# High weights against both parts of the rows in one 512-column product, in the gate and up chunks of a feed-forward block

## The reference

```
def swiglu(h, w_gate, w_up, w_down):
    return (jax.nn.silu(h @ w_gate) * (h @ w_up)) @ w_down

f = swiglu(rms_norm(h, ffn1_pre_g[l]), ffn1_w_gate[l], ffn1_w_up[l], ffn1_w_down[l])
h = h + FFN_RESIDUAL_SCALE * rms_norm(f, ffn1_post_g[l])
```

## Time and profile before

| what | value |
|---|---|
| time, median of 3 runs | 1905.47 us (1904.33 to 1905.68) |
| the profiled execution | 1905.51 us, its span 1903.5 us |
| mean granted TensorE clock | 0.951 of full speed |
| PE busy | 1800.9 us (95%), 12512 matmuls |
| DVE busy | 1123.6 us (59%) |
| ACT busy | 793.8 us (42%) |
| DMA | 297.33 MB, mean 156 GB/s |

### The profile page before, as it was taken

The page is one execution under the profiler, slowest core; times in us unless marked ns, Lnnn a source line. Parts: engine busy times, 40 slices in busy tenths (PEclk is TensorE's granted clock), DMA queues, the critical chain, the costliest instruction groups (busy, mean ns, idle before and its releaser), DMA issues.

```text
span 1903.5 us, 28797 instructions
## 1 busy us (share of the span) xinstructions
PE 1800.9 (95%) x12512; PEld 1667.4 (88%) x12512; DVE 1123.6 (59%) x1315; ACT 793.8 (42%) x1009; POOL 42.6 (2%) x64
## 2 busy tenths in 40 slices
PE   7999997999999999999999799999999998879987
PEld 6999897898898999899989789889899987668765
DVE  5444689654357444744568965435744478647763
ACT  5333633443345333533353345334533454444442
POOL 0000000000000000000000000000000010001000
PEclk9999999798899999999999979979999999889979
DMA  7555544233255555545555423324555553215210
GB/s 276 178 194 182 199 178 155 89 133 133 90 177 199 179 192 182 204 179 190 186 196 181 155 89 133 133 89 166 194 195 178 191 201 123 89 44 209 96 66 22
DMA packets 43037, 297.33 MB, mean 156 GB/s; under 512 B 4768, under 2 KB 5152, under 8 KB 8352
## 3 DMA queue, kind: packets, MB, share of 16 engines
q1 hardware_dynamic: 39744, 285.23, 41.4%
q10 hardware_dynamic: 3168, 10.26, 1.5%
HBM read 294.42 MB, written 1.05 MB: 155 GB/s over the span
## 4 chain that ended last, share of the span: by engine, by line
PE 75%; DVE 10%; ACT 6%; issue 5%; DVEq 2%; POOL 1%; DMA 1%; ACTq 0%; POOLq 0%; SPq 0%
PE ps L1347 21%; PE ps L1348 21%; PE ps L1349 21%; DVE wlo L816 3%; DVE mix L1015 2%; ACT whi L525 2%; PE ps L1715 2%; PE ps L1742 2%; PE ps L1579 1%; PE ps L1574 1%; ACT prob L786 1%; PE ps L1433 1%; PE ps L1581 1%; POOL rs L486 1%; PE ps L1726 1%
## 5 line engine op out<-in xcount | busy, mean ns | idle before, releaser
L816 DVE TENSOR_TENSOR wlo<-raw,whi 128x2048 fp32r<-128x2048 f32 x270 | 616.5, 2290 | 445.8 <-ACT whi L525 434.3
L1347 PE MATMUL ps<-xhi,whi 128*128 128x256 f32 x2496 | 724.9, 290 | 5.2 <-DVE wlo L816 5.0
L1348 PE MATMUL ps<-xlo,whi 128*128 128x256 f32 x2496 | 717.5, 287 | 0.0
L1349 PE MATMUL ps<-xhi,wlo 128*128 128x256 f32 x2496 | 716.8, 287 | 0.0
L525 ACT ACTIVATE whi<-raw 128x2048 fp32r<-128x2048 f32 x270 | 509.2, 1906 | 17.5 <-DMA raw<-stream 16.9
L1347 PEld LDWEIGHTS ps<-xhi,whi 128*128 128x128 f32 x2496 | 491.4, 197 | 15.4 <-DVE wlo L816 7.0
L1348 PEld LDWEIGHTS ps<-xlo,whi 128*128 128x128 f32 x2496 | 491.0, 197 | 2.6 <-issue 0.6
L1349 PEld LDWEIGHTS ps<-xhi,wlo 128*128 128x128 f32 x2496 | 490.4, 196 | 0.0
L1347 PE MATMUL ps<-whi,yar 128*128 128x512 f32 (+1 forms) x492 | 195.9, 398 | 0.7 <-DVE wlo L816 0.7
L1348 PE MATMUL ps<-wlo,yar 128*128 128x512 f32 (+1 forms) x492 | 192.1, 390 | 0.0
L1349 PE MATMUL ps<-whi,yar 128*128 128x512 f32 (+1 forms) x492 | 191.4, 389 | 0.0
(11 more groups left out here) (202 smaller groups left out, 1896.8 us busy)
## 6 DMA issues: line engine op xcount, KB each, us to landing
raw<-stream SPq DMA_DIRECT2D x270, 1024.0 KB, 4.8
gpre<-pre_gain ACTq DMA_DIRECT2D x9, 512.0 KB, 4.2
gpost<-post_gain ACTq DMA_DIRECT2D x6, 512.0 KB, 5.0
h<-x_in SPq DMA_DIRECT2D x2, 512.0 KB, 5.9
out<-mix SPq DMA_DIRECT2D x4, 256.0 KB, 2.0
cst<-cst_in ACTq DMA_DIRECT2D x1, 704.0 KB, 12.1
cst<-cst_in ACTq DMA_DIRECT2D x1, 576.0 KB, 6.7
par<-par ACTq DMA_DIRECT2D x2, 271.0 KB, 5.5
```

The lines of the kernel that those rows point to most:

```text
L816: TT(wlo[:, s, :], raw[:, s, :], whi[:, s, :].bitcast(F32), ALU.subtract).then_inc(lo_v, 1)
L1347: pe.matmul(dst, lh, rh, start=first, stop=False)
L1348: pe.matmul(dst, lh, rl, start=False, stop=False)
L1349: return pe.matmul(dst, ll, rh, start=False, stop=last)
```

## The change

`xhi` and `xlo` become the two halves of one tile `xhl`, side by side for each slice k. For groups 2 to 10 of every feed-forward stage (18 chunks a stage, 72 in all), `features_wide` takes the place of `features`: the high weights multiply both halves in one matmul of 512 columns, then the low weights multiply the high half in one of 256 columns into the first half of the same bank. Each half m has now a bank of its own: gate goes to banks 2 and 3, up to banks 0 and 1. The sum of the two halves of each bank is left to DVE, as a reduction over pairs: `gate_sum` in the second half of `thb`, `up_sum` in the second half of `tmp`. ACT takes silu of `gate_sum` instead of PSUM. TensorE waits for the reductions of the group before instead of silu and product.

```diff
+            def features_wide(ch, b):
+                s = ch % SLOTS
+                wh, wl = wts(whi, s, KD), wts(wlo, s, KD)
+                for m in range(2):
+                    w = slice(m * P, (m + 1) * P)
+                    for k in range(KD):
+                        pe.matmul(bank(b + m), wh[:, k, w], xhl[:, k, :, :].rearrange("p a t -> p (a t)"),
+                                  start=(k == 0), stop=False)
+                        ins = pe.matmul(bank(b + m)[:, 0:T], wl[:, k, w], xhi[:, k, :], start=False, stop=(k == KD - 1))
+                ins.then_inc(used, 1)
...
                 def gate_up(c, g):
                     ready(c)
-                    pe.wait_ge(silu_done, f * NG + g)
-                    features(c, 0)
+                    if g > 2:
+                        pe.wait_ge(gate_done, f * (NG - 2) + (g - 2))
+                    features_wide(c, 2)
                     ready(c + 1)
-                    pe.wait_ge(prod_done, f * NG + g)
-                    features(c + 1, 1)
+                    if g > 2:
+                        pe.wait_ge(up_done, f * (NG - 2) + (g - 2))
+                    else:
+                        pe.wait_ge(prod_done, f * NG + 2)
+                    features_wide(c + 1, 0)
...
             def ffn(ch, f):
+                def gate(c, g):
+                    if g < 2:
+                        return
+                    chunk_used(dve, c)
+                    dve.wait_ge(silu_done, f * NG + g)
+                    dve.tensor_reduce(gate_sum, ps[:, 2:4, :].rearrange("p m (a t) -> p m t a", a=2), AX,
+                                      ALU.add).then_inc(gate_done, 1)
+
                 def up(c, g):
+                    if g < 2:
+                        dve.wait_ge(silu_done, f * NG + g + 1)
+                        chunk_used(dve, c)
+                        TT(prod, silu, bank(1), ALU.mult).then_inc(prod_done, 1)
+                        return
+                    chunk_used(dve, c)
+                    dve.tensor_reduce(up_sum, ps[:, 0:2, :].rearrange("p m (a t) -> p m t a", a=2), AX,
+                                      ALU.add).then_inc(up_done, 1)
+                    dve.drain()
                     dve.wait_ge(silu_done, f * NG + g + 1)
-                    chunk_used(dve, c)
-                    TT(prod, silu, bank(1), ALU.mult).then_inc(prod_done, 1)
+                    TT(prod, silu, up_sum.rearrange("p m t -> p (m t)"), ALU.mult).then_inc(prod_done, 1)
...
                 for g in (NG - 2, NG - 1):
                     c = ch + FFN_CH - 7 + 2 * (g - (NG - 2))
+                    gate(c, g)
                     split(c + 3)
                     up(c + 1, g)
                     hidden(g)
...
                 def silu_of(g, c):
-                    chunk_used(act, c)
+                    if g < 2:
+                        chunk_used(act, c)
+                    else:
+                        act.wait_ge(gate_done, f * (NG - 2) + (g - 1))
                     if g:
                         act.wait_ge(prod_done, f * NG + g)
-                    A(silu, bank(0), ACT.Silu).then_inc(silu_done, 1)
+                    src = bank(0) if g < 2 else thb[:, 512:1024]
+                    A(silu, src, ACT.Silu).then_inc(silu_done, 1)
```

More of the change, by code:

```diff
@@ L236, in program @@
         h = sb("h", [P, NT, D])
-        xhi = sb("xhi", [P, KD, T], F32R)
-        xlo = sb("xlo", [P, KD, T], F32R)
+        xhl = sb("xhl", [P, KD, 2, T], F32R)
+        xhi, xlo = xhl[:, :, 0, :], xhl[:, :, 1, :]
         mix = sb("mix", [P, 11456])
@@ L300, in program @@
         th2 = thb[:, 512:1024]
+        gate_sum = thb[:, 512:1024].rearrange("p (m t) -> p m t", m=2)
+        up_sum = tmp[:, 512:1024].rearrange("p (m t) -> p m t", m=2)
         lat_hi = yar[:, 0, 0:768].rearrange("p (m t) -> p m t", m=3)
@@ L360, in program @@
         prod_done = sem("prod_done")
+        gate_done = sem("gate_done")
+        up_done = sem("up_done")
         ht_done = sem("ht_done")
```

## The result

| | before | after |
|---|---|---|
| time, median (range, runs) | 1905.54 us (1902.65 to 1913.18, 8) | 1915.33 us (1911.08 to 1919.01, 8) |
| ratio, 95% interval | | 1.0049 (1.0031 to 1.0066) |
| profiled execution | 1905.51 us, span 1903.5 | 1915.33 us, span 1913.5 |
| mean granted clock | 0.951 | 0.949 |

A forecast was written before the change was run, and what follows sets the result against it. The prediction took TensorE's pace, busy 95% of the span, as the bound. It summed 1905.51 - 15.6 + 12.6 + 3.9 = 1906.4 us, likeliest range 1902 to 1910, 8 in 10 from 1899 to 1917.

The forecast's parts named there:

- PE in the 72 wide chunks: TensorE in groups 2 to 10: a chunk takes 5.54 us instead of 5.76, saving 15.6 us in four stages.
- I take the rows' value: Wide chunks' 512-column matmul: assumed 0.2265 us, as in down chunks, though no row showed it with alternating bank halves.
- DVE and ACT in groups 2 to 8: Two added reductions a group, 1.22 us each, are hidden in the 16.55 us period and cost nothing.
- The last two groups: Groups 9 and 10 of each stage: reductions delay the last down chunk's split, 3.15 us a stage, +12.6 us.
- Nothing is won back: Stage end: after the late last split, DVE's boundary and TensorE both move by the same 3.15 us.
- The clock: TensorE's 3.5 us wait at stage ends drops the clock, 1.3 us in three of four stages, +3.9 us.
- Slow reduction: Rival, DVE in the last two groups: a reduction over pairs takes 2.29 us, giving 1923.5 us; chance 0.12.
- fast reduction: Rival, stage ends: a reduction takes 0.69 us, TensorE waits only 1.6 us, clock holds, 1894.8 us; chance 0.10.
- The clock holding: Rival: the clock stays full through the waits at stage ends, giving 1902.5 us; chance 0.20.
- The wide matmul saving nothing: Rival, wide chunks: they stay at 5.76 us, the fixed part not being saved, giving 1919.5 us; chance 0.08.
- The estimate from the Trainium skill: Merging two matmuls saves about 2.5 ns each over 1152 matmuls, 2.9 us; it spoke against the change.
- the likeliest case: The forecast itself for the whole kernel, 1906.4 us, own range 1902 to 1910 us; chance 0.50.

The follow-up runs named there:

- e4: The changed kernel with each half's 8 matmuls of 512 columns together, then its 8 of 256, instead of turn about; 1909.63 us, ratio 1.0025 to the kernel before.
- e5: The changed kernel with the narrow matmul adding into the second half of its bank instead of the first; 1915.78 us, one run.
- e6: The changed kernel with weight splits ahead in groups 9 and 10 and low weights multiplying both halves, so all wide-chunk matmuls have 512 columns; 2010.49 us, one run.
- e1: The changed kernel with wide products in groups 2 to 8 only, groups 9 and 10 as before; 1897.99 us, ratio 0.996 to the kernel before.
- e2: The changed kernel with wide products in groups 9 and 10 only, groups 2 to 8 as before; 1924.46 us, ratio 1.009 to the kernel before.
- e3: The changed kernel, all 72 chunks wide, with weight splits ahead of silu and reduction in groups 9 and 10; 1894.03 us, ratio 0.9945 to the kernel before.
- e7: The kernel before with only the weight splits moved ahead in groups 9 and 10, no wide products; 1900.75 us, ratio 0.9981.
- e8: The changed kernel with weight splits ahead in groups 9 and 10 and equal-length matmuls grouped; 1889.26 us, ratio 0.9919 to the kernel before.
- run 232: Not an experiment: "run" is a verb here, and 232 ns is the first of the wide steps listed for e4's first stage.

## Why the prediction was right or wrong

- **PE in the 72 wide chunks (-15.6 us): wrong in size.** The step that failed is "I take the rows' value": 0.2265 and 0.120 us, read from chunks of one length each, for two lengths turn about. Measured is 352.9 ns a pair, so 5.65 us a chunk instead of 5.54, and 72 x 0.113 = 8.1 us saved. The groups of 16.79 us show another small part: 5.50 us are left for the down chunk beside wide ones, against 5.46. The bounds held the value, and e4, e5 and e6 give the cause. The trace of before had shown it already: in its first stage a down chunk, which follows 256-column matmuls, steps on average at 233, 235, 229, 233 and 231 ns before it settles at 227, and in e6, where all lengths are equal, at 226 or 227 from its first step. The mean of 0.2275 held these steps; to take 0.2265 was to leave out what the wide chunks would meet at every matmul.
- **DVE and ACT in groups 2 to 8 (nothing): right.** The reduction takes 1.22 us, no wait appears there, and e1's four stages win 5.2 us, what PE's steps alone give (6.3 less the down chunks' 1.0).
- **The last two groups (+12.6 us): right, a little less.** Counted from the end of gate 9 (171.63, that is 0.27 ahead of the first reduction), the working put the last split at 194.89 and it stood at 194.99; all DVE steps between agree within 0.11 us. As the chunks were slower than forecast, TensorE came later and waited less: 8.68 - 5.82 = 2.86 us a stage, 11.4 in all. e1 and e2 show that this is the loss, e3 that it is order and not work. "Nothing is won back" behind it held: the boundary on DVE starts right behind the three splits, as before.
- **The clock (+3.9 us): right in kind.** It fell in two of four stages, not three. Stages 2 and 3 are equal before and 1.34 us apart after; I take this as the price of one such stretch, for which I had 1.3. In e5, where it fell in stages 1, 3 and 4, stages 3 and 4 are only 0.9 longer than stage 2, so the price is 0.9 to 1.3. Over the four kernels with the wait (after, e2, e4, e5) it fell in 13 of 16 stages, and in none of the 20 stages of e1, e3, e6, e7 and e8, nor in the four of before. That it would fall in some stages and not in others was a guess, and what decides it stays open.
- **The sum.** With measured sizes 11.4 + 2.7 - 8.1 + 1.1 (the down chunks, 4 x 7 x 0.04) = 7.1 us for the stages, and 7.1 were found, 7.3 with the start of the kernel. The remaining 2.8 us of the 10.1 lie in parts that the change doesn't touch and were in no term; they are inside the spread of those parts. The forecast's terms came to 0.9 us, and the first one alone, sized twice too large, makes 7.5 us of the difference. That the time still fell inside the range is owed to the range's width, and not to the sum.
- **Rivals.** Slow reduction and fast reduction: both fell by the 1224 ns. The clock holding: it held in two stages only. The wide matmul saving nothing: half true, since about half of the expected saving is missing, but for a cause that the rival did not name. The estimate from the Trainium skill (TensorE: Matmul & The Clock Gate, section "Wait — 56ns, not 53.3ns?", 2.9 us in all) doesn't agree either: 8.1 us were saved in the steps.
- **The chances** put 0.59 on no change and 0.26 on slower, with 1909.3 us as the edge; slower came, though no rival that stood for it did. It came by a saving half as large, and the likeliest case's range was too narrow for its first term.

## What to carry to other kernels

When an edit adds work to an engine with 40% to spare, look for the place where that engine and others wait for each other in turn and the engine that decides the time has least other work to go on with; two reductions a group were free in the 28 groups of the loop here and cost 2.9 us at each of four ends. If the delay there is a queue's order, put what has no unfinished input (here, the weight splits) ahead of what has. A step read from a run of equal matmuls does not hold for a mix of lengths; group equal lengths.

## What the runs showed of the hardware

Equal matmuls follow each other at 120 ns (256 columns) and 226.7 ns (512), each with its own weight load. Turn about, they take 236.0 and 116.8: 6.3 ns a pair more. In groups of eight the loss is 1.7 ns a pair: in e4's first stage the wide steps run 232, 234, 228, 231, 230 and then 227 ns, the narrow ones 113, 119 and then 120, so the pace settles only some matmuls behind a change. What in TensorE causes it was not settled; which half of the bank is written (e5) and the operands of the wide chunks as such (e6) are ruled out. A TensorE wait with a step of 3.4 to 3.6 us over it, between dense stretches, was followed by a stretch of 3.4 us (once, in e4, 6.8) at 1.2 GHz in 13 of 16 places. The kernels in which one stage has it and another has not put its price at 0.9 to 1.3 us.
